# Attention 1 with unscaled probabilities and one division per pair of heads

## The chip, the cores and the metric

One Trainium2 chip, one core. The metric is device time in microseconds of one launch, median of several runs; the profile is one more execution, recorded by the hardware profiler. Engines are called PE (matmul), PEld (its weight loads), DVE (VectorE), ACT (ScalarE), POOL (GpSimd) and SP (SyncE, which only issues weight DMAs here).

## The reference

512 positions, width 1024, float32 throughout. A first block (adaptive modulation, token mixer, convolutional feed-forward) is followed by two more layers (windowed attention with a sink, then latent attention), each with a gated side input. The change lies in the token mixer's attention: 8 heads of 64, chunks of 64 positions, each query sees its own chunk and the 8 before it.

```python
z = h @ w_in + b_in
q, k, v, glu_a, glu_b, gate_a, gate_b = jnp.split(z, splits, axis=-1)
scores = einsum(qc, kb) * HEAD_DIM ** -0.5 + bias      # masked with -1e30
probs = softmax(scores, axis=-1)
out = einsum(probs, vb)
a = out.reshape(b, s, D_ATTN) @ w_attn_o
u = causal_dwconv(glu_a * sigmoid(glu_b), w_dw, b_dw)  # 31 taps, 512 channels
cb = silu(layer_norm(u, g_ln, b_ln)) @ w_conv_o + b_conv_o
y = sigmoid(gate_a) * a + sigmoid(gate_b) * cb
```

The value's share of `b_in` is a constant per channel; rows of `probs` sum to one, so it may be added to v or to `out`.

## The kernel before

All activations stand with channels on the 128 partitions and the 512 positions along the free dimension. Every matmul product is made of three (`mm3`, L610 to L612): each operand is split into a high part in fp32r and the low rest, and hi*hi, hi*lo and lo*hi are added in PSUM. Weights stream from HBM in chunks of 128x1024 by SP's queue; for each chunk ACT makes the high part (`split`, L1029) and then DVE the low one (L1484). PE waits for DVE's count.

The first attention runs in `pair_attention`, a loop over 32 steps (8 heads times 4 query tiles of 128), written out once for each engine and tied by semaphores. Steps go in pairs: step i even and i+1 are the two heads of a pair at the same query tile t; tile t has t+1 key tiles of 128, so widths run 128, 128, 256, 256, 384, 384, 512, 512 and then again. Eight steps finish one pair of heads. What each engine does, by step i:

- PE: at even i the scores of both heads (`pair_scores`, L702), which need the maxima up to step i-1; then two blocks of the gates' matmul (`first_gates`); then the product with the values of step i-5 for odd tiles (`half_values`); then the transposes of the probabilities of step i-3 (`turn`, L732), which wait for the scaled probabilities and for DVE's lo of step i-5; then two more gate blocks. Four blocks a step make one gate tile in two steps, 16 tiles in all. After step 17 `conv_mean` (L817) and after steps 21 and 23 `conv_square` (L824) sum over channels for the layer norm.
- DVE: at even i the masked, biased, negated scores and their minimum for step i (`pair_maxima`, L1587); the reciprocal of the sum of step i-1 (`inverse`, L1599); the low part of the turned probabilities of step i-3 (`pair_turn_lo`, L1615); at odd i the scaling of the probabilities of step i-1 (`norms`, L1609); at even i the maxima of step i+1; at i = 9, 13, ... half an output out of PSUM with the value bias added (`out1`, L1728, two instructions); then `mixer_step`: at even i the low half of a weight chunk, and two of the convolution's taps (`conv_taps`, L1561, 33 of them fall into this loop, the last at step 16) or parts of the layer norm; at i = 15, 23, ... the low part of a finished pair's output (`out1_lo`, L1497).
- ACT: the high part of the turned probabilities of step i-3 (`pair_turn_hi`, L1112); the exponential of step i with its row sum (`exps`, L1087); at even i the scaling of the probabilities of step i-1 (`norms`, L1098); then at even i a gate's tanh (L1239) and a weight chunk's high part (L1029), at odd i a product for the modulation (`ada_product`, L1249); every eighth step the high part of a pair's output (L1034).
- POOL: adds the products of ACT, 128x1024 each, into an accumulator (L520), one in each odd step, and fetches the next.

So even-numbered steps' probabilities are scaled by DVE and odd-numbered ones' by ACT, both in place and before they are turned.

PSUM has 8 banks: 4 and 5 hold scores, 6 and 7 turned probabilities. The other four (`LIN`) are a ring: every output tile of PE takes the next bank in the order in which tiles are finished (`mixer_tiles` for this loop), and `free_bank` makes its first matmul wait until the tile four places earlier has been read. The list `evicted` holds, tile by tile, the semaphore and count that tell so.

The third attention (`attention3`) already leaves its probabilities unscaled: ACT writes the row sums to `lsum`, DVE inverts those of two heads in one instruction (`invert_sums`), copies each over 64 columns (`spread_inverses`, L2032, a 128x512 copy), PE turns that in four transposes (`inverses`, L990) and DVE multiplies the pair's output by the turned inverses out of PSUM (`normalise`, L2040).

## Time and profile before

| | us |
|---|---|
| median of 3 runs (two of them 1616.49 and 1616.67, one 2873.28) | 1616.67 |
| the profiled execution | 1618.08 |
| span of its instructions | 1616.3 |
| PE busy | 1468.8 (91%) |
| DVE busy | 988.3 (61%) |
| ACT busy | 732.9 (45%) |
| POOL busy | 236.7 (15%) |
| PE on the chain that ended last | 70% |
| first attention, from its first scores (198.4) to its last values (365.5) | 167.1 |

Busy time counts an instruction from its start to its modelled end; matmuls overlap, so a PE that is busy all the time can still have slack inside it. The chain that ended last is followed back from the last instruction to whatever released each step. The two sound runs agree within 0.2 us, and the profiled one took 1.4 us more than they.

### The profile page before, as it was taken

What the parts mean: (1) busy time and instruction counts of PE and PEld (TensorE: products, weight loads), DVE (VectorE), ACT (ScalarE), POOL (GpSimd) and SP (SyncE); (2) the same over time, 40 slices, a digit from 0 to 9 for tenths busy, and PEclk for the clock granted to TensorE, in tenths of its full rate; (3) what the DMA queues carried; (4) which work ended last, traced back from release to release, by engine and by line L of the source; (5) the groups of instructions that cost most, each with busy time, mean ns of one, the idle gap of its engine ahead of it and who ended that gap; (6) DMA issues with size and microseconds to landing.
All of it is one profiled execution on the core that took longest, in us unless ns stands there. A gap on an engine that the chain in (4) does not pass through costs nothing.

```text
span 1616.3 us, 19654 instructions
## 1 busy us (share of the span) xinstructions
PE 1468.8 (91%) x6834; PEld 1156.0 (72%) x6834; DVE 988.3 (61%) x1549; ACT 732.9 (45%) x1265; POOL 236.7 (15%) x218
## 2 busy tenths in 40 slices
PE   5898797979987999999998999998999989999897
PEld 3686575767765888887885677776777768778775
DVE  5669878465755555554223647984562568788454
ACT  4424454562324455454123426774442446666442
POOL 3105623231110000000000000111110012222111
PEclk8999799988998999999999999998999999999999
DMA  9532133324621232323322321112222120000221
GB/s 388 192 103 88 56 105 111 110 92 172 219 78 28 102 101 80 104 85 99 102 91 65 98 91 60 59 47 92 80 90 79 55 89 14 27 27 27 105 80 64
DMA packets 39881, 151.65 MB, mean 94 GB/s; under 512 B 4784, under 2 KB 4928, under 8 KB 39040
## 3 DMA queue, kind: packets, MB, share of 16 engines
q1 hardware_dynamic: 29664, 105.92, 20.0%
q0 software_dynamic: 10144, 44.76, 7.6%
q8 instruction: 45, 0.74, 0.2%
q14 instruction: 28, 0.23, 0.0%
HBM read 144.37 MB, written 6.29 MB: 93 GB/s over the span
## 4 chain that ended last, share of the span: by engine, by line
PE 70%; DVE 16%; ACT 7%; issue 5%; DMA 1%; DVEq 0%; POOL 0%; ACTq 0%; SPq 0%; POOLq 0%
PE ps L610 21%; PE ps L611 20%; PE ps L612 20%; DVE w_lo L1484 2%; PE ps L732 2%; PE ps L667 2%; DVE c_acc L1561 2%; ACT w_hi L1029 2%; DVE p L1609 1%; PE ps L702 1%; DMA w_raw<-in_w 1%; PE ps L687 1%; DVE minus_s L1587 1%; DVE pt_lo L1615 1%; DVE tmp L1688 1%
## 5 line engine op out<-in xcount | busy, mean ns | idle before, releaser
L610 PE MATMUL ps<-a_hi,w_hi 128*128 128x512 f32 x880 | 362.3, 412 | 19.7 <-ACTq L1308 11.8
L611 PE MATMUL ps<-a_lo,w_hi 128*128 128x512 f32 x880 | 351.1, 399 | 0.0
L612 PE MATMUL ps<-a_hi,w_lo 128*128 128x512 f32 x880 | 351.0, 399 | 0.0
L1484 DVE TENSOR_TENSOR w_lo<-w_raw,w_hi 128x1024 fp32r<-128x1024 f32 x130 | 166.4, 1282 | 159.6 <-ACT w_hi L1029 158.9
L610 PEld LDWEIGHTS ps<-a_hi,w_hi 128*128 128x128 f32 x880 | 167.9, 191 | 63.6 <-ACTq L1308 12.7
L612 PEld LDWEIGHTS ps<-a_hi,w_lo 128*128 128x128 f32 x880 | 167.6, 190 | 40.2
L611 PEld LDWEIGHTS ps<-a_lo,w_hi 128*128 128x128 f32 x880 | 167.9, 191 | 35.4 <-issue 0.5
L1029 ACT ACTIVATE w_hi<-w_raw 128x1024 fp32r<-128x1024 f32 x138 | 144.4, 1048 | 70.9 <-PE ps L612 55.0
L610 PE MATMUL ps<-b_hi,w_hi 128*128 128x512 f32 x240 | 99.3, 414 | 10.5 <-DVE b_lo L1858 5.6
L611 PE MATMUL ps<-b_lo,w_hi 128*128 128x512 f32 x240 | 96.6, 403 | 0.0
L612 PE MATMUL ps<-b_hi,w_lo 128*128 128x512 f32 x240 | 96.5, 402 | 0.0
L732 PE MATMUL ps<-ident,p 128*128 128x128 f32 x496 | 84.2, 282 | 10.7 <-DVE p L1609 10.4
L1561 DVE SCALAR_TENSOR_TENSOR c_acc<-u_pad,vecs,c_acc 128x512 f32<-128x512 f32 x90 | 85.5, 999 | 0.2
L732 PEld LDWEIGHTS ps<-ident,p 128*128 128x128 f32 x496 | 59.1, 142 | 29.7 <-DVE p L1609 14.0
L1044 ACT ACTIVATE sq<-x_resid 128x512 f32<-128x512 f32 x56 | 35.2, 631 | 98.9 <-DVE x_resid L1937 62.9
L1824 DVE SCALAR_TENSOR_TENSOR c_gate<-u_ff,vecs,c_gate 128x512 f32<-128x512 f32 x44 | 32.9, 748 | 64.4 <-ACT u_ff L1329 64.4
L610 PE MATMUL ps<-g_hi,w_hi 128*128 (+1 forms) x176 | 69.5, 395 | 1.5 <-issue 1.5
L611 PE MATMUL ps<-g_lo,w_hi 128*128 (+1 forms) x176 | 69.4, 394 | 0.0
L612 PE MATMUL ps<-g_hi,w_lo 128*128 (+1 forms) x176 | 69.4, 394 | 0.0
L536 POOL TENSOR_TENSOR sq<-sq 128x512 f32<-128x512 f32 x30 | 38.8, 1293 | 185.9 <-ACT sq L1044 185.9
L1615 DVE TENSOR_TENSOR pt_lo<-ps,pt_hi 128x256 fp32r<-128x256 f32 (+3 forms) x96 | 45.8, 478 | 31.5 <-ACT pt_hi L1112 31.4
L610 PEld LDWEIGHTS ps<-b_hi,w_hi 128*128 128x128 f32 x240 | 46.3, 193 | 24.1 <-issue 6.7
(306 smaller groups left out, 2999.8 us busy)
## 6 DMA issues: line engine op xcount, KB each, us to landing
w_raw<-in_w SPq DMA_DIRECT2D x198, 512.0 KB, 3.5
ada_a<-in_ada POOLq DMA_DIRECT2D x16, 512.0 KB, 7.8
ada_g<-in_ada POOLq DMA_DIRECT2D x16, 512.0 KB, 3.8
ada_b<-in_ada POOLq DMA_DIRECT2D x16, 512.0 KB, 4.3
x_resid<-in_x POOLq DMA_DIRECT2D x2, 2048.0 KB, 11.9
pl_store<-pl_out POOLq DMA_DIRECT2D x2, 2048.0 KB, 8.7
pl<-pl_store POOLq DMA_DIRECT2D x2, 2048.0 KB, 8.7
alibi<-in_alibi POOLq DMA_DIRECT2D x16, 192.0 KB, 2.7
```

The source lines that it names most:

```text
L536: pool.tensor_tensor(sq[:, 0, :], sq[:, 0, :], sq[:, 1, :], ALU.add).then_inc(sq_used, 1)
L610: pe.matmul(o, w[0], r[0], start=start, stop=False, skip_group_check=skip)
L611: pe.matmul(o, w[0], r[1], start=False, stop=False, skip_group_check=skip)
L612: return pe.matmul(o, w[1], r[0], start=False, stop=stop, skip_group_check=skip)
L667: pe.matmul(ps[:, STAT_BANK, :], ones[:, :], sq[:, q % 2, :], start=(k == 0), stop=(k == n - 1)).then_inc(sq_used, 1)
L732: m = pe.transpose(ps[:, T_BANK + n % 2, P * s:P * s + P], a.p[:, n % 4, a.p_at + P * (s - b):a.p_at + P * (s - b) + P], ident[:, :])
L1029: act.activation(w_hi[:, n % SLOTS, :], w_raw[:, n % RAW, :], ACT.Copy).then_inc(w_hi_done, 1)
L1044: act.activation(sq[:, slot, :], src, ACT.Square).then_inc(sq_ready, 1)
L1484: dve.tensor_tensor(w_lo[:, n % SLOTS, :], w_raw[:, n % RAW, :], w_hi[:, n % SLOTS, :].bitcast(F32), ALU.subtract).then_inc(w_lo_done, 1)
L1561: dve.scalar_tensor_tensor(c_acc[:, f, :], src, w, c_acc[:, f, :], ALU.mult, ALU.add).then_inc(conv_step, 1)
L1615: dve.tensor_tensor(lo_, ps[:, T_BANK + n % 2, turned].rearrange("p (s q) -> p s q", q=P), hi.bitcast(F32), ALU.subtract).then_inc(pt_read ...
L1824: dve.scalar_tensor_tensor(c, u_ff[:, 2 * pair + j, tap:tap + TOK], vecs[:, bass.ds(i * 2 + (VO["w_dwf"] + tap * 2 * FT + w_at + pair), 1) ...
```

## The change

It takes the third attention's way of dividing over to the first. Shared helpers get the attention as an argument (`inverses`, `invert_sums`, `spread_inverses`); for the first, the row sums go to `lsum`, DVE inverts a pair's at the end of step 8, 16, 24, 32, spreads them at the end of step 9, 17, 25, 33, PE turns them at the end of step 11, 19, 27, 35, and DVE multiplies at step 13, 21, 29, 37. `inverse` and `norms` stay in the second attention only. The value bias is added by ACT with the high part and again by DVE with the low part. PE's turn now waits for the exponential itself.

```diff
-LN_SUM, LN_SUB, LN_SQUARE, LN_SCALE, LN_OUT = 17, 19, 20, 25, 28
+LN_SUM, LN_SUB, LN_SQUARE, LN_SCALE, LN_OUT = 17, 18, 20, 25, 28
@@ mixer_tiles
+        if i % 8 == 3 and i >= 11:
+            order.append(("l", i // 8 - 1))
@@ eviction of the first attention's tiles
-            evicted.append({"o": (R["o1_half"], j // 2 + 1) if j % 2 == 0 else (tmp_w, tmps_ahead + j // 2 + 1), "g": (R["gate_t"], j + 1), "mean": (R["ln_mean"], CT),
+            evicted.append({"o": (R["o1_half"], j + 1), "l": (tmp_w, tmps_ahead + j + 1), "g": (R["gate_t"], j + 1), "mean": (R["ln_mean"], CT),
@@ attn1 (where the spread inverses stand, by pair)
+                     lambda pair: tile1["l", pair], lambda pair: rs[:, (0, 2, 0, 1)[pair], :], 0)
@@ PE, turn
-                elif n % 2 == 1:
-                    pe.wait_ge(p_ready_act, n // 2 + 1)
+                elif a is attn1:
+                    pe.wait_ge(e_done, n + 1)
                 else:
-                    pe.wait_ge(p_ready, n // 2 + 1)
+                    pe.wait_ge(p_ready_act if i % 2 else p_ready, i // 2 + 1)
@@ PE, pair_attention
                     after(i)
+                    if a is attn1 and i % 8 == 3 and i >= 11:
+                        inverses(a, i // 8 - 1)
@@ ACT, exps and pair_attention
+                least, total = col[:, 0, c:c + 1], col[:, 1, c:c + 1] if a is attn2 else lsum[:, h // 2 % 2, h % 2, t:t + 1]
+                if a is not attn2 and t == 0 and h % 2 == 0 and h >= 4:
+                    act.wait_ge(l_inv, a.pairs_ahead + h // 2 - 1)
-                    if 0 <= i - 1 < a.steps:
+                    if a is attn2 and 0 <= i - 1 < a.steps:
                         norms(a, i - 1)
@@ ACT, high part of a pair's output: Copy becomes Identity with the value bias
+                act.activation(qk_hi[:, pair, :], tmp[:, tmps[0] % 2, :], ACT.Identity, bias=v("b_in", BI_V + pair)).then_inc(hi_done, 1)
@@ DVE, pair_maxima in the second attention
-                        if h >= 2:
-                            dve.wait_ge(e_done, n - 1)
+                    if i >= 2:
+                        dve.wait_ge(e_done, n - 1)
@@ DVE, pair_attention
-                    if 0 <= i - 1 < a.steps:
-                        inverse(a.n0 + i - 1)
+                    if a is attn2 and 0 <= i - 1 < a.steps:
+                        inverse(a, i - 1)
...
-                    if 0 <= i - 1 < a.steps:
+                    if a is attn2 and 0 <= i - 1 < a.steps:
                         norms(a, i - 1)
...
+                    if a is attn1 and i % 8 == 5 and i >= 13:
+                        divide1(i // 8 - 1)
                     after(i)
+                    if a is attn1 and i % 8 == 0 and i >= 8 and i <= a.steps:
+                        invert_sums(a, i // 8 - 1)
+                    if a is attn1 and i % 8 == 1 and i >= 9:
+                        spread_inverses(a, i // 8 - 1)
@@ DVE, out1 (tensor_scalar with the bias becomes tensor_copy), out1_lo
+                    m = dve.tensor_copy(tmp[half(h), tmps[0] % 2, q], src[half(h), 2 * P * h:2 * P * h + 2 * P])
+                dve.scalar_tensor_tensor(qk_lo[:, pair, :], tmp[:, (tmps[0] - 1) % 2, :], v("b_in", BI_V + pair),
+                                         qk_hi[:, pair, :].bitcast(F32), ALU.add, ALU.subtract).then_inc(R["o1"], 1)
@@ DVE, new
+            def divide1(pair):
+
+                inv = bank(attn1.inv(pair))
+                dve.wait_ge(R["o1_half"], 2 * pair + 2)
+                slot = tmp_slot()
+                dve.tensor_tensor(slot, slot, inv, ALU.mult).then_inc(tmp_w, 1)
```

`LN_SUB` is the first of the two steps in which DVE subtracts the mean from the convolution's result (two channel tiles in each).

## Rows read from the trace of the kernel before

**Rows 1.** Windows, core 0, stages of the first attention: busy us (count), TensorE clock, DMA.
```profile
198.00:282.00 84.00, 72.13 (x355) 55.54 (x356) 64.03 (x125) 42.58 (x86) 22.00 (x18) 0.95 0.31 101
...
288.00:330.00 42.00, 42.00 (x225) 32.67 (x226) 22.13 (x52) 25.14 (x49) 9.41 (x7) 1.00 0.28 90
330.00:357.00 27.00, 19.60 (x105) 14.83 (x105) 18.82 (x43) 18.59 (x36) 8.25 (x5) 0.97 0.35 117
357.00:372.00 15.00, 11.51 (x50) 10.45 (x51) 5.30 (x12) 6.01 (x10) 3.99 (x4) 0.50 0.30 105
```

**Rows 2.** Timeline of ACT inside one loop: start us, us, engine, line, op, names, shape.
```profile
266.06 0.72 ACT L1087 ACTIVATE p<-p,col 128x512 f32<-128x512 f32 x1 [6.71 <-DVE col L1587]
...
266.79 0.60 ACT L1098 ACTIVATE p<-p,col 128x384 f32<-128x384 f32 x1
267.29 0.66 ACT L1239 ACTIVATE x_resid<-ps,halves 128x512 f32<-128x512 f32 x1
267.86 1.05 ACT L1029 ACTIVATE w_hi<-w_raw 128x1024 fp32r<-128x1024 f32 x1
```

**Rows 3.** Timeline of DVE, an earlier stall and then the same loop.
```profile
258.35 3.76 DVE L1561 SCALAR_TENSOR_TENSOR c_acc<-u_pad,vecs,c_acc 128x512 f32<-128x512 f32 x2
...
268.94 1.23 DVE L1484 TENSOR_TENSOR w_lo<-w_raw,w_hi 128x1024 fp32r<-128x1024 f32 x1 [1.91 <-ACT w_hi L1029]
270.08 1.53 DVE L1561 SCALAR_TENSOR_TENSOR c_acc<-u_pad,vecs,c_acc 128x512 f32<-128x512 f32 x2
271.53 0.16 DVE L1599 RECIPROCAL col<-col 128x1 f32<-128x1 f32 x1
271.61 0.54 DVE L1615 TENSOR_TENSOR pt_lo<-ps,pt_hi 128x384 fp32r<-128x384 f32 x1
272.06 2.23 DVE L1609 TENSOR_SCALAR p<-p,col 128x512 f32<-128x512 f32 x1
274.21 1.53 DVE L1561 SCALAR_TENSOR_TENSOR c_acc<-u_pad,vecs,c_acc 128x512 f32<-128x512 f32 x2
...
276.25 0.28 DVE L1587 CUSTOM_DVE_ANT_0 p<-ps,rel 128x128 f32<-128x128 f32 x1
```

**Rows 4.** Timeline of POOL over the same stretch.
```profile
259.17 2.38 POOL L520 TENSOR_TENSOR acc_g<-acc_g,ada_g 128x1024 f32<-128x1024 f32 x1 [6.81 <-ACT ada_g L1249]
...
271.64 2.37 POOL L520 TENSOR_TENSOR acc_g<-acc_g,ada_g 128x1024 f32<-128x1024 f32 x1 [9.21 <-ACT ada_g L1249]
```

**Rows 5.** Lines by form, ACT, 198 to 360 us: count | busy us, mean ns | idle.
```profile
L1098 ACT ACTIVATE p<-p,col 128x512 f32<-128x512 f32 x4 | 2.8, 711 | 3.0 <-DVE col L1599 3.0
...
L1098 ACT ACTIVATE p<-p,col 128x128 f32<-128x128 f32 x4 | 1.6, 388 | 0.0
```

**Rows 6.** Lines by form, DVE, 198 to 360 us.
```profile
L1609 DVE TENSOR_SCALAR p<-p,col 128x512 f32<-128x512 f32 x4 | 7.3, 1813 | 0.0
```

**Rows 7.** Tile sq in the third attention: count, duration ns min/median/max, first and last start.
```profile
L990 PE MATMUL ps<-ident,sq x32: 269/272/277, 1355.7 to 1504.8; 128*128 128x128 f32 x32
...
L2032 DVE COPY sq<-gvec x8: 416/418/420, 1351.4 to 1502.8; 128x512 f32<-128x512 f32 x8
```

**Rows 8.** Tile o_pair in the third attention.
```profile
L2040 DVE TENSOR_TENSOR o_pair<-o_pair,ps x8: 676/678/686, 1363.0 to 1505.4; 128x512 f32<-128x512 f32 x8
```

**Rows 9.** Timeline of PE at three places, with idle time before in brackets.
```profile
281.23 3.75 PE L817 MATMUL ps<-c_acc,ones 128*128 128x512 f32 x4 [4.82 <-issue]
...
304.24 1.88 PE L824 MATMUL ps<-sq,ones 128*128 128x512 f32 x4
...
356.90 1.11 PE L732 MATMUL ps<-ident,p 128*128 128x128 f32 x4 [6.32 <-DVE p L1609]
```

**Rows 10.** Timeline of DVE where PE runs without a pause.
```profile
305.26 0.41 DVE L1615 TENSOR_TENSOR pt_lo<-ps,pt_hi 128x256 fp32r<-128x256 f32 x1
305.58 0.41 DVE L1609 TENSOR_SCALAR p<-p,col 128x384 f32<-128x384 f32 x1
305.91 0.97 DVE L1728 TENSOR_SCALAR tmp<-ps,vecs 64x256 f32<-64x256 f32 x2
```

More of the change, by code:

```diff
@@ L417, in build @@
                      lambda h, s: (vb_hi[:, s, P * (h // 2):P * (h // 2) + P], vb_lo[:, s, P * (h // 2):P * (h // 2) + P]),
-                     p3, (pt3_hi, pt3_lo), full, lambda h: tile3["o", h], [[(s, 0, 2) for s in range(4)], [(s, 2, 4) for s in range(4)]])
+                     p3, (pt3_hi, pt3_lo), full, lambda h: tile3["o", h], [[(s, 0, 2) for s in range(4)], [(s, 2, 4) for s in range(4)]],
+                     lambda pair: tile3["l", pair], lambda pair: sq[:, pair % 2, :], H1 // 2)
         used_at = {}
@@ L733, in turn, with inverses @@
                 m.then_inc(t_done, 1)
+            def inverses(a, pair):
+                o = free_bank(a.inv(pair))
+                pe.wait_ge(l_rows, a.pairs_ahead + pair + 1)
+                for t in range(NT):
+                    m = pe.transpose(o[:, P * t:P * t + P], a.spread(pair)[:, P * t:P * t + P], ident[:, :])
+                m.then_inc(lin_done, 1)
             def pair_attention(a, after, between=None):
@@ L983, in value_tile @@
                 m.then_inc(lin_done, 1)
-            def inverses(pair):
-                o = free_bank(tile3["l", pair])
-                pe.wait_ge(R["l_rows"], pair + 1)
-                for t in range(NT):
-                    m = pe.transpose(o[:, P * t:P * t + P], sq[:, pair % 2, P * t:P * t + P], ident[:, :])
-                m.then_inc(lin_done, 1)
             def own_head(h):
@@ L1003, in mla_piece @@
                     elif kind == "l":
-                        inverses(head)
+                        inverses(attn3, head)
                     else:
@@ L1593, in maxima3, with inverse, invert_sums, spread_inverses @@
                 dve.tensor_reduce(col[:, 0, n % 4:n % 4 + 1], ps[:, S_BANK + n % 2, :], AX.X, ALU.max, negate=True).then_inc(m_ready, 1)
-            def inverse(n):
-                c = n % 4
+            def inverse(a, i):
+                n = a.n0 + i
                 dve.wait_ge(e_done, n + 1)
-                dve.reciprocal(col[:, 2, c:c + 1], col[:, 1, c:c + 1]).then_inc(r_ready, 1)
+                dve.reciprocal(col[:, 2, n % 4:n % 4 + 1], col[:, 1, n % 4:n % 4 + 1]).then_inc(r_ready, 1)
             def norms(a, i):
+                if i % 2:
+                    return
                 n = a.n0 + i
-                if n % 2 == 1:
-                    return
                 b, e = a.spans[a.step(i)[1]]
                 p = a.p[:, n % 4, a.p_at:a.p_at + P * (e - b)]
-                dve.wait_ge(r_ready, n + 1)
+                dve.wait_ge(r_ready, i + 1)
                 dve.tensor_scalar(p, p, col[:, 2, n % 4:n % 4 + 1], None, ALU.mult).then_inc(p_ready, 1)
+            def invert_sums(a, pair):
+                dve.wait_ge(*((s_free, 2 * NT * (pair + 1)) if a is attn3 else (e_done, a.n0 + 2 * NT * (pair + 1))))
+                if pair >= 2:
+                    dve.wait_ge(l_rows, a.pairs_ahead + pair - 1)
+                dve.reciprocal(linv[:, pair % 2, :, :], lsum[:, pair % 2, :, :]).then_inc(l_inv, 1)
+            def spread_inverses(a, pair):
+                dve.wait_ge(l_inv, a.pairs_ahead + pair + 1)
+                if pair >= 2:
+                    dve.wait_ge(lin_done, a.inv(pair - 2) + 1)
+                dve.tensor_copy(a.spread(pair).rearrange("p (t e d) -> p t e d", t=NT, e=2),
+                                linv[:, pair % 2, :, :].rearrange("p e t -> p t e").unsqueeze(3).to_broadcast([P, NT, 2, HD])
+                                ).then_inc(l_rows, 1)
             def pair_turn_lo(a, i):
@@ L1724, in out1 @@
             def out1(j):
-                src, c = bank(attn1.lin(j)), VO["b_in"] + BI_V + j // 2
+                src, q = bank(attn1.lin(j)), slice(2 * P * (j % 2), 2 * P * (j % 2) + 2 * P)
                 for h in range(2):
-                    m = dve.tensor_scalar(tmp[half(h), tmps[0] % 2, 2 * P * (j % 2):2 * P * (j % 2) + 2 * P],
-                                          src[half(h), 2 * P * h:2 * P * h + 2 * P], vecs[half(h), c:c + 1], None, ALU.add)
-                m.then_inc(tmp_w if j % 2 else R["o1_half"], 1)
-                tmps[0] += j % 2
+                    m = dve.tensor_copy(tmp[half(h), tmps[0] % 2, q], src[half(h), 2 * P * h:2 * P * h + 2 * P])
+                m.then_inc(R["o1_half"], 1)
             def out1_lo(pair):
-                lo_of_tmp(qk_lo[:, pair, :], qk_hi[:, pair, :], R["o1"])
+                his[0] += 1
+                dve.wait_ge(hi_done, his[0])
+                dve.scalar_tensor_tensor(qk_lo[:, pair, :], tmp[:, (tmps[0] - 1) % 2, :], v("b_in", BI_V + pair),
+                                         qk_hi[:, pair, :].bitcast(F32), ALU.add, ALU.subtract).then_inc(R["o1"], 1)
             def mixer_step(i):
```

59 lines of the change are left out of this document (24 added, 35 removed).

## The prediction

> **What bounds the kernel now.** I read the windows first, then the timelines of ACT, DVE and POOL inside a loop of the first attention, then the groups by form. The windows (columns: stretch, its length, busy us of PE, PEld, DVE, ACT, POOL with counts, TensorE's clock as a share of 2.4 GHz, DMA) cut the attention into four stages [rows 1]. From 198 to 282 us, steps 0 to 17, PE is busy 72 of 84 us, so it has holes; from 288 to 330, steps 18 to about 27, it is busy all 42; from 330 to 357 it has holes again, 7.4 us; from 357 to 372 it runs at 0.50, that is at 1.2 GHz. The change can gain only where PE has holes, and anything that it gives PE to do or to wait for between 288 and 330 counts in full.
>
> What makes the holes is a loop between ACT and DVE, two steps long. ACT waits 6.71 us for DVE's maxima, then does the exponential (266.06), scales the odd step's probabilities (266.79), does a gate's tanh (267.29) and a weight chunk's high part (267.86) [rows 2]. DVE waits for that chunk: its low part starts at 268.94, then two taps, a reciprocal, a lo, the scaling of the even step's probabilities (272.06), two more taps, and the next maxima at 276.25 [rows 3]. So one turn of 10 us has one of ACT's scalings and one of DVE's in it. What DVE does ahead of its wait of 1.91 us (the other reciprocal, the other lo) is covered.
>
> **DVE against POOL.** The scaling at 272.06 took 2.23 us. POOL's addition ran from 271.64 to 274.01, and DVE's next instruction began at 274.21 [rows 3, 4]. The same width costs 1.8 us on average [rows 6], a 384 wide one away from POOL 0.41 [rows 10]. A pair of taps at 258.35 took 3.76 us instead of 1.53, and POOL was adding from 259.17 to 261.55 [rows 3, 4]. The lo of 271.61, which reads PSUM, took its usual 0.54 beside the same addition. So what is held is an instruction whose inputs are all in SBUF, and it is held whichever it is. With the scaling gone, the tap behind it is held until 274.01. Such a place gives 0.2 us, not 2.2. The rows stand for four such scalings (steps 4, 6, 8, 14) and two such pairs of taps (steps 10, 12) up to 282 us. The Trainium skill says the same in "SBUF — State Buffer", section "Who interferes with whom": a single-input VectorE instruction in a two-port mode, or one with two SBUF inputs, and GpSimd lock each other out for a whole instruction. Were the hold the scaling's own, the four held ones of this stretch would give 7 us more, and the sum below would be 1604; the trace bears out the rule.
>
> **The sum, part by part.**
>
> Steps 2 to 17 (until the taps end and PE can sum the mean), gains. ACT's scalings last 388 ns at width 128 and 711 at 512 [rows 5]; neighbours overlap by 0.1 (266.79 plus 0.60 is 267.39, the next starts at 267.29 [rows 2]). That is 0.29 to 0.61, mean 0.45, times 8: 3.6 us. DVE's scalings on the path are 7: three unheld ones at about 0.33 (305.58 to 305.91 [rows 10]), four held ones at 0.2: 1.8 us. At step 9 the half output, which reads PSUM, moves up beside POOL's addition: 0.5 us. Reciprocals on the path: 271.53 to 271.61 is 0.08 [rows 3], times 7: 0.6 us. Together 6.5.
>
> Costs in the same stretch, all on DVE in the loop: an inversion of 8 columns at step 8, like a reciprocal, 0.15; a spread at step 9, 0.42 in the third attention [rows 7], 0.35 behind another; a division at step 13, 0.68 in the third attention [rows 8], 0.6 behind another. Together 1.1. Net gain to the mean: 5.4 us. The tensor_copy for the tensor_scalar of the half output, and the bias in ACT's and DVE's last instructions, keep shape and engine: nothing. The spread reads and writes SBUF, so it can be held by POOL's 2.4 us like the scaling was; at step 9 it stands behind two taps, after the addition, and I count nothing. Bounds of the four spreads: 0.35 each, or 0.42 plus 2.4 each.
>
> PE must still keep up. It is idle 4.82 us before the mean [rows 9] and for the rest of its 12 us of holes before that [rows 1]; 5.4 us fit. Four transposes of 272 ns each, overlapping to some 0.13 apart, are 0.5 us per pair [rows 7]; those of step 11 fall into a hole.
>
> The mean. PE's idle time before it stays near 4 us, because DVE and ACT set both its ends. The clock should fall there as before. I count no change.
>
> Steps 18 to 24, PE without a hole. The four transposes of step 19 cost 0.5. Then the ring. The new tile of each pair takes a bank, and is freed by DVE's division, so the tile four places later waits for it: that is the third pair's first output half at step 15 (tile 11 behind 7), the variance at step 21 (19 behind 15), and the seventh half at step 31 (27 behind 23). At step 21 PE came to the squares at 304.24 [rows 9]; DVE's lo was at 305.26 and its half output at 305.91, 0.97 long [rows 10]. In the new order DVE no longer subtracts two means in step 20 (1.2 us, moved to 18) and ACT has no scaling (0.5), but PE's own turn is 0.5 late: lo at about 304.2, half output to 305.5, division to 306.15. PE arrives at 304.24 + 0.53 = 304.8. It waits 1.4 us. With `LN_SUB` at 18 the mean's bank is free as PE wants it at step 20, within 0.3 us; with 19 it would be a step late. Cost of the stretch: 1.9 us. Bounds of the wait: 0, if DVE comes earlier, and 3, if POOL's addition holds DVE ahead of it.
>
> At steps 15 and 31 PE waits 1.5 us more for its bank, but after both it has a hole of that size or more: in step 16 it needs DVE's maxima, as ACT does at 266.06 [rows 2], and after step 32 it stood idle for 6.32 us [rows 9]. Nothing. If that cover went, it would be 1.5 each.
>
> Steps 24 to 31, the loop bounds again. Each turn gives ACT's 0.3 to 0.5, DVE's 0.2 to 0.33 and a reciprocal. Against them stand the inversion and spread at steps 24 and 25, and the division at 29. Turn by turn: 0.1, 0.6, 0.2. Gain 0.9.
>
> Tail. PE waited until 356.90 for the scaling at step 30 [rows 9], and again until ACT had scaled step 31. Both waits go; late next is the lo of step 29, behind a held `out1_lo` on DVE (the addition of POOL holds that one in the scaling's stead, so 0.25 earlier). The last turns come 1.2 us earlier and the values follow; the last transposes (0.5 to 0.9 at this clock) and the last division (0.65) come onto the chain that ends with `out1_lo` and releases the next stage. Net gain 1.2.
>
> Second attention: one more wait per step in front of the maxima, always satisfied, since the reciprocal of the step before has waited for the same count: nothing. Third attention: the spread waits for PE's transposes two pairs back instead of its own multiply: nothing.
>
> Sum: 5.4 - 1.9 + 0.9 + 1.2 = 5.6 us. From the profiled execution's 1618.1 that gives 1612.5; that execution stood 1.4 above the median of 1616.67, from which the same sum gives **1611.1 us**. That is 0.35%; about 2% is what a measurement of this kernel can tell from no change.
>
> **The rivals.**
>
> *The clock stays up.* PE's pause at 350.6 shrinks from 6.32 us to about 4, and what runs from 357 to 372 at 1.2 GHz may then run at 2.4. For it: the pause shrinks. Against it: in the same stretch PE is busy in small pieces only, and the pause before the mean hardly shrinks. PE is busy 11.5 us there [rows 1], half of which would go, less what waits for others: some 4.5 us, 1606.5; with the mean's stretch as well (the four matmuls of the row at 281.23 take 3.75 us [rows 9], all eight some 7, and half would go), 1603.
>
> *The ring of banks decides: slower.* Each division holds a bank that PE wants two or three steps later, and it comes behind a lo and a half output on DVE. If PE's holes are not where I put them, the three waits (1.5 each), the transposes (2.1), the four spreads and inversions (2.0) and the last division (0.65) all land: 9.3 us against gains of 6.5 + 1.5 + 0.5 = 8.5. Time 1617.5. One held spread makes it 1620. It decides from the point at which PE's waits for its bank add up to more than 0.8 us per turn of the loop, what ACT and DVE save in one. For it: in steps 18 to 24 PE has no hole at all. Against it: DVE waits 1.9 us for ACT even in a loop turn that it bounds.
>
> *Nothing moves.* The loop's saving is eaten by POOL's additions: they start a fixed time after ACT's product, and if DVE comes earlier, its taps start inside them more often, each held up to 2.2 us. Two such would leave 1615.
>
> **How the numbers follow.** Forecast as summed, 1609 to 1614: 0.55. Clock up: 0.15. Ring, slower: 0.15. Nothing moves: 0.15. The range for 8 in 10 leaves out the best end of the clock's case and the worst of the ring's: 1604 to 1618. Over 2% is 32 us, several times every gain or cost named here: faster 0.01, slower 0.01, within 0.98.
>
> **What would show it.** Right: no L1609 or L1098 before 900 us; the mean's matmuls start near 276 instead of 281; the taps behind a lo now show the 2 us that the scalings had; a wait of 1 to 1.5 us before the first squares, released by DVE's division; the pause of 6.3 us down to about 4. Wrong: spreads longer than 0.5 us; pauses of PE at steps 15 or 31 that end later than the loop does; scores still 10 us apart in steps 6 to 16; a different clock between 357 and 372.

## The result, and the profile after

| | before | after | |
|---|---|---|---|
| median, us | 1617.35 | 1607.49 | -9.9 |
| lowest and highest | 1615.1 to 1618.5, and one of 2873.28 | 1606.81 to 1609.37 | six runs each |
| ratio | | 0.9944 | 95% interval 0.9930 to 0.9958 |
| profiled execution | 1618.08 | 1606.92 | -11.2 |
| span, mean granted clock | 1616.3, 0.956 | 1605.1, 0.963 | |

One of the six runs of before took 2873.28 us; the median of before counts it and the ratio does not, so the gain is 9.9 by the medians and 9.1 by the ratio. In the later comparisons before had medians of 1617.2 to 1618.8. The forecast was 1611.1, with a gain of 5.6, and within 2% of no change; so it is, and the interval leaves out no change.

The windows of [rows 1] for the kernel after (columns as there):

```profile
198.00:282.00 84.00, 78.55 (x374) 59.30 (x373) 63.09 (x107) 39.33 (x78) 26.21 (x23) 0.92 0.37 117
288.00:330.00 42.00, 39.50 (x207) 29.87 (x206) 20.82 (x43) 23.99 (x44) 9.35 (x7) 1.00 0.31 101
330.00:357.00 27.00, 21.85 (x122) 18.04 (x120) 19.77 (x36) 16.79 (x32) 10.63 (x6) 0.87 0.30 98
357.00:372.00 15.00, 12.02 (x54) 10.28 (x54) 4.54 (x9) 4.04 (x7) 1.62 (x3) 0.77 0.28 105
```

PE does 78.5 us of work up to 282 us instead of 72.1. The stage without holes begins and ends earlier, so the window of 288 to 330 now has the first of the next stage's. And the last window runs at 0.77 of the full clock instead of 0.50: in before the clock was at its lower level from 355.6 to 376.0, in after from 347.7 to 354.5 and from 361.4 to 368.2. In the first window it is the other way round, 0.92 for 0.95: after lost it in the mean (below) and from 259.0 to 265.8, at the end of a wait for the division at step 15:

```profile
259.48 0.55 PE L617 MATMUL ps<-pt_hi,v_hi 128*128 128x256 f32 x1 [2.81 <-DVE tmp L1801]
```

Before waited 1.26 us at that place. Nothing on DVE waits for PE between there and the mean, so the 1.55 more fell into a hole.

The same loop of DVE as in [rows 3], five microseconds earlier, from its timeline:

```profile
264.93 1.53 DVE L1572 SCALAR_TENSOR_TENSOR c_acc<-u_pad,vecs,c_acc 128x512 f32<-128x512 f32 x2
266.38 0.55 DVE L1643 TENSOR_TENSOR pt_lo<-ps,pt_hi 128x384 fp32r<-128x384 f32 x1
266.85 3.47 DVE L1572 SCALAR_TENSOR_TENSOR c_acc<-u_pad,vecs,c_acc 128x512 f32<-128x512 f32 x2
...
274.42 0.74 DVE L1572 SCALAR_TENSOR_TENSOR c_acc<-u_pad,vecs,c_acc 128x512 f32<-128x512 f32 x1
...
275.75 0.84 DVE L1762 COPY tmp<-ps 64x256 f32<-64x256 f32 x2
276.63 1.23 DVE L1635 COPY rs<-gvec 128x512 f32<-128x512 f32 x1
```

And POOL's two additions of that stretch:

```profile
266.58 2.40 POOL L527 TENSOR_TENSOR acc_g<-acc_g,ada_g 128x1024 f32<-128x1024 f32 x1 [8.83 <-ACT ada_g L1260]
...
275.24 2.34 POOL L527 TENSOR_TENSOR acc_g<-acc_g,ada_g 128x1024 f32<-128x1024 f32 x1 [5.39 <-ACT ada_g L1260]
```

The scaling is gone, and the pair of taps behind the lo takes 3.47 us instead of 1.53: its first tap is held until the addition ends at 268.98, as the scaling of 272.06 was in [rows 3]. The half output at 275.75 (L1762, out of PSUM) runs beside the next addition in its usual 0.84; the spread behind it (L1635, SBUF to SBUF) takes 1.23 instead of 0.42.

PE around the mean, before the squares and at the last turns, from its timeline:

```profile
275.26 5.37 PE L834 MATMUL ps<-c_acc,ones 128*128 128x512 f32 x8 [2.64 <-issue]
```

```profile
298.94 1.98 PE L841 MATMUL ps<-sq,ones 128*128 128x512 f32 x4 [1.39 <-DVE tmp L1801]
```

```profile
348.18 1.09 PE L739 MATMUL ps<-ident,p 128*128 128x128 f32 x4 [2.29 <-DVE pt_lo L1643]
351.43 0.87 PE L739 MATMUL ps<-ident,p 128*128 128x128 f32 x3 [2.16 <-DVE pt_lo L1643]
```

The mean starts at 275.3 instead of 281.2. The wait of 1.39 us for the division is new. The 6.32 us in front of the turn of step 30 [rows 9] have become 2.29 and 2.16, both until a lo of DVE. DVE at that place:

```profile
347.48 0.55 DVE L1643 TENSOR_TENSOR pt_lo<-ps,pt_hi 128x384 fp32r<-128x384 f32 x1
347.94 2.87 DVE L1768 SCALAR_TENSOR_TENSOR qk_lo<-tmp,vecs,qk_hi 128x512 fp32r<-128x512 f32 x1
350.73 0.55 DVE L1643 TENSOR_TENSOR pt_lo<-ps,pt_hi 128x384 fp32r<-128x384 f32 x1
```

The `out1_lo` at 347.94 takes 2.87 us instead of 0.75 behind POOL's addition, and the lo on which PE waits stands behind it.

How the lead over before grew, each place read from PE's timeline in both kernels:

| place | before | after | lead | lead without the 0.9 of the start | forecast |
|---|---|---|---|---|---|
| first scores | 198.4 | 197.4 | 0.9 | 0 | 0 |
| mean's matmuls | 281.2 | 275.3 | 6.0 | 5.1 | 5.4 |
| scores of step 18 | 287.8 | 280.6 | 7.3 | 6.4 | 5.4 |
| scores of step 24 | 315.7 | 310.5 | 5.2 | 4.3 | 3.5 |
| maxima of step 30 (DVE) | 347.9 | 342.0 | 5.9 | 5.0 | 4.4 |
| first product of the next stage | 368.0 | 360.0 | 8.0 | 7.1 | 5.6 |
| end of the span | 1616.3 | 1605.1 | 11.2 | 10.3 | 5.6 |

The 0.9 us at the start counts as scatter: kernels that do not differ up to there had their first scores between 197.4 and 199.1.

### The profile page after: what moved, and what is told of

Its sections match the earlier page's. It is cut to its first block, busy times and chain, and to the rows that moved or that the text cites. A ratio compares the mean times of both kernels' runs of the same rounds, so it can differ in the third digit from the quotient of the medians.

```text
span 1605.1 us, 19696 instructions
## 1 busy us (share of the span) xinstructions
PE 1464.9 (91%) x6850; PEld 1153.0 (72%) x6850; DVE 984.4 (61%) x1513; ACT 726.8 (45%) x1249; POOL 236.5 (15%) x218
## 4 chain that ended last, share of the span: by engine, by line
PE 69%; DVE 16%; ACT 7%; issue 6%; DMA 1%; POOL 0%; DVEq 0%; ACTq 0%; SPq 0%; POOLq 0%
PE ps L617 21%; PE ps L618 20%; PE ps L619 20%; PE ps L739 2%; DVE w_lo L1495 2%; ACT w_hi L1038 2%; DVE c_acc L1572 2%; PE ps L674 1%; PE ps L709 1%; DMA w_raw<-in_w 1%; DVE minus_s L1599 1%; DVE p L1621 1%; PE ps L694 1%; DVE tmp L1722 1%; DVE a_lo L1727 1%
## 5 line engine op out<-in xcount | busy, mean ns | idle before, releaser
L617 PE MATMUL ps<-a_hi,w_hi 128*128 128x512 f32 x880 | 362.0, 411 | 20.6 <-ACTq L1319 11.8
L1572 DVE SCALAR_TENSOR_TENSOR c_acc<-u_pad,vecs,c_acc 128x512 f32<-128x512 f32 x90 | 91.8, 1068 | 0.2
L1120 ACT ACTIVATE pt_hi<-ps 128x256 fp32r<-128x256 f32 (+3 forms) x96 | 41.0, 427 | 53.2 <-PE ps L739 53.0
```

The source lines that it names most:

```text
L617: pe.matmul(o, w[0], r[0], start=start, stop=False, skip_group_check=skip)
L1120: act.activation(hi, ps[:, T_BANK + n % 2, turned].rearrange("p (s q) -> p s q", q=P), ACT.Copy).then_inc(pt_hi_done, 1)
L1572: dve.scalar_tensor_tensor(c_acc[:, f, :], src, w, c_acc[:, f, :], ALU.mult, ALU.add).then_inc(conv_step, 1)
```

## The experiments

Eleven kernels ran beside before, and one more at the end; kernels on the same chip shared their runs of before. The table is for looking up; the runs follow in the order of the questions.

| run | median, us | ratio to before, 95% |
|---|---|---|
| x1_removal | 1604.39 | 0.9922 (0.9907 to 0.9937) |
| x2_act_load | 1616.96 | 1.0003 (0.9990 to 1.0016) |
| x3_dve_load | 1614.97 | 0.9984 (0.9974 to 0.9993) |
| x4_squares_later | 1607.25 | 0.9939 (0.9927 to 0.9951) |
| x5_before_small_adds | 1600.90 | 0.9900 (0.9885 to 0.9914) |
| x6_after_small_adds | 1599.17 | 0.9887 (0.9873 to 0.9902) |
| x7_filler | 1605.41 | 0.9925 (0.9912 to 0.9939) |
| x8_filler_squares | 1602.77 | 0.9907 (0.9893 to 0.9922) |
| x9_before_filler | 1612.47 | 0.9969 (0.9959 to 0.9980) |
| x10_adds_at_maxima | 1597.56 | 0.9877 (0.9862 to 0.9892) |
| x12_before_adds_at_maxima | 1601.53 | 0.9903 (0.9888 to 0.9918) |
| x11_all | 1590.95 | 0.9835 (0.9819 to 0.9852) |

### What the removal and the additions are worth

**x1_removal** takes the scalings and reciprocals out and adds nothing: no inversion, no spread, no turned inverses, no division, so that the first attention's outputs stay unscaled. The mean is subtracted at step 19 again, and the ring of banks is that of before.

```diff
-                        inverses(a, i // 8 - 1)
...
-                        divide1(i // 8 - 1)
...
-                        invert_sums(a, i // 8 - 1)
-                        spread_inverses(a, i // 8 - 1)
```

> Scalings and reciprocals of the first attention are left out and nothing is put in their place (no inversion, spread, transposes or division, so this attention's outputs stay unscaled; mean subtracted at step 19 and the bank ring as before). Theory: what the change adds costs 1.1 us in steps 2 to 17, 1.9 in steps 18 to 24 (half of it a wait of PE for the variance's bank), about 1.1 in steps 24 to 31 and 1 in the tail, so this is 4 to 5 us faster than the changed kernel: about 1603 us, and PE shows no pause before the first squares. Rival, the additions are hidden: as fast as the changed kernel, 1607 to 1608.

Measured 1604.39: 3.1 us under after, where 4 to 5 were expected. Counted from the first scores, its lead over after in the profile is 0.9 at the mean, 2.6 at the scores of step 18, 4.7 at step 24 and 5.8 at the first product of the next stage. But 1.7 of that are the clock inside the mean, whose eight matmuls take 5.37 in after:

```profile
274.70 3.67 PE L830 MATMUL ps<-c_acc,ones 128*128 128x512 f32 x8 [3.37 <-issue]
```

Without it the additions cost 0.9 before the mean (1.1 forecast), 2.1 up to step 24 (1.9) and 1.1 behind (some 2). Of the lead, 2.6 are lost again behind the attention, where the code is the same but for a wait in the third attention; see the clock below.

**x2_act_load** is after with ACT's 16 scalings put back as work without use (same widths and places, into a scratch tile of bfloat16); **x3_dve_load** is after with DVE's 16 scalings and 32 reciprocals put back in the same way.

```diff
+                    if a is attn1 and i % 2 == 0 and 0 <= i - 1 < a.steps:
...
+                        act.activation(scr[:, 0:wd], a_hi[:, 0, 0:wd].bitcast(F32), ACT.Copy, scale=c_act[:, 0:1]).then_inc(scr_done, 1)
```

```diff
+                        dve.reciprocal(col[:, 2, i % 4:i % 4 + 1], ones[:, 0:1])
...
+                        dve.tensor_scalar(scr[:, 0:wd], a_hi[:, 0, 0:wd].bitcast(F32), c_act[:, 0:1], None, ALU.mult)
```

> The changed kernel with ACT's 16 scalings put back as work that nobody waits for (same widths and place, read from another tile, written to a spare one in bfloat16). Theory: ACT's scaling lies on the loop between ACT and DVE; 3.6 us back in steps 2 to 17 and about 1.5 in steps 24 to 31: 1612 us, scores of step 16 some 3.5 us later. Rival, ACT's share was covered by DVE and only PE's waits counted: no change, 1607 to 1608.

> The changed kernel with DVE's 16 scalings and 32 reciprocals put back as work that nobody waits for (written to a spare tile in bfloat16). Theory: an instruction that POOL's addition holds gives its hold over to the next one with its inputs in SBUF, so putting the scalings back costs only their own 0.2 to 0.33 and the reciprocals 0.08: 2.5 to 3.5 us, 1611, while the summed time of the taps falls by about the 5 to 8 us that the put-back scalings show above 0.4 each. Rival, the hold is the scaling's own: 8 us or more, 1616, with the taps as long as in the changed kernel.

At the mean both came as expected: it starts 3.1 us later than in after with ACT's load (3.6 forecast) and 2.9 later with DVE's (2.5 to 3.5). At the end they cost 9.5 and 7.5 (6.5 by the ratios), where some 5 and 3.5 were expected: the totals lie near the rivals of both forecasts. Together they are far more than the whole change gave: the two gains are not a sum, and with either load back most of the whole is gone. DVE's timeline in x3_dve_load, the same loop again:

```profile
267.47 1.53 DVE L1573 SCALAR_TENSOR_TENSOR c_acc<-u_pad,vecs,c_acc 128x512 f32<-128x512 f32 x2
...
269.45 2.34 DVE L1668 TENSOR_SCALAR scr<-a_hi,c_act 128x512 bf16<-128x512 f32 x1
271.71 1.53 DVE L1573 SCALAR_TENSOR_TENSOR c_acc<-u_pad,vecs,c_acc 128x512 f32<-128x512 f32 x2
```

The load's scaling at 269.45 takes the hold of POOL's addition (2.34 us), and the pair of taps behind it is back at 1.53. From the start of the first pair of taps to the end of the second it is 5.77 us here, 5.66 in before and 5.39 in after: the held scaling and its reciprocal cost 0.3 to 0.4 us and not 2.2. The same holds over the whole loop. These are the 33 taps of after and of x3_dve_load, as groups by form from 198 to 360 us (count, busy us, mean ns, idle):

```profile
L1572 DVE SCALAR_TENSOR_TENSOR c_acc<-u_pad,vecs,c_acc 128x512 f32<-128x512 f32 x33 | 34.3, 1068 | 0.2
```

```profile
L1573 DVE SCALAR_TENSOR_TENSOR c_acc<-u_pad,vecs,c_acc 128x512 f32<-128x512 f32 x33 | 28.1, 878 | 0.2
```

Six holds of taps in after are two in x3_dve_load, and the taps take 6.2 us less, as expected (5 to 8); 28.1 and 878 are also their numbers in before. This is shown, then: the hold passes to what follows.

What is beyond 3 us comes behind that. x2_act_load is 3.6 late at the scores of step 18, 5.8 at step 24, 7.0 at step 30 and 10 past the first product of the next stage; its profiled execution, 1621.07, was one of the slower of its runs (1613.09 to 1621.62), so that its profile shows more than the median. PE's time for the mean's eight matmuls is 6.69 us in before, 5.37 in after, 5.92 and 6.07 in these two, and 3.67 in x1_removal. The pause before the squares is 1.79 us in x2_act_load instead of 1.39, and the clock falls in the squares (303.4 to 306.8): the four matmuls take 3.51 us instead of 1.98.

### POOL's additions

**x5_before_small_adds** and **x6_after_small_adds**: before and after, with POOL adding 8 columns of 1024, which leaves the modulation incomplete.

```diff
-                    pool.tensor_tensor(acc[:, :], acc[:, :], ada_g[u % 2][:, :], ALU.add).then_inc(ada_g_used, 1)
+                    pool.tensor_tensor(acc[:, 0:8], acc[:, 0:8], ada_g[u % 2][:, 0:8], ALU.add).then_inc(ada_g_used, 1)
```

> The kernel before, with POOL's 14 additions for the modulation cut from 1024 to 8 columns (the modulation of two groups comes out incomplete). Theory: the holds go, 1.7 to 2.2 us at each of six places up to 282 us, but PE's own 8 us a turn then bounds: the mean 7 to 9 us earlier, 2 more at the layer norm's scaling and 2 at the last scalings: 1604 to 1607. Rival, the holds were covered: above 1612.

> The changed kernel with the same cut additions. Theory: the changed kernel is held at the same six places, by its taps, so it gains too, but it is nearer to PE's bound: the mean about 5 us earlier, 2 each at the layer norm's scaling and at the low part of the third pair's output: 1597 to 1600, 5 to 8 us below the kernel before with cut additions. Rival, holds belonged to the scalings: it gains under 3 us, 1605, and the change is worth nothing without POOL's additions.

Before fell by 16 us (10 to 13 were expected) and after by 8.3, so that only 1.7 us lie between them (the intervals of the two ratios overlap) instead of 5 to 8. Without the holds the scalings cost before little: its mean starts 71.9 us after the first scores, against 70.5 in x6_after_small_adds, 77.8 in after and 82.9 in before. PE's window in x6_after_small_adds says why (columns as in [rows 1]):

```profile
198.00:282.00 84.00, 81.90 (x419) 63.50 (x421) 57.44 (x118) 44.04 (x87) 10.29 (x23) 0.97 0.37 122
288.00:330.00 42.00, 40.60 (x211) 30.56 (x210) 22.38 (x47) 26.60 (x50) 3.03 (x8) 1.00 0.31 102
```

PE is busy 81.9 of 84 us, it bounds the stage, and what DVE saves behind it buys little. In the profiles x6_after_small_adds leads x5_before_small_adds by 1.5 at the mean, 3.1 at the scores of step 18 (1.7 of it the mean's clock), 0.6 at those of step 30 and, with the shorter pauses of the tail, 4.0 at the first product of the next stage. So 8 to 16 us of the kernel hang on the holds, more than on the scalings.

**x10_adds_at_maxima** keeps all additions and all other work and only places them: POOL waits until the maxima of the step are through before it adds, so that its 2.4 us lie under DVE's reading of PSUM and its wait for ACT. **x12_before_adds_at_maxima** is the same wait in before.

```diff
                 if k:
+                    pool.wait_ge(*((m_ready, 2 * u + 5) if u < 14 else (pt_ready, NT * H1)))
```

> The changed kernel with each of POOL's additions held back until the maxima of the next even step are done (and the last two until the last low part is), so that they run while DVE reads PSUM and waits for ACT. All work stays. Theory: the holds go as with the cut additions; up to 1599.2 as measured there, less what still meets a tap: 1600 to 1602. Rival: an addition of 2.4 us behind the maxima now holds the weight chunk's low part, 1.9 us behind them, in every turn: no gain, 1607, or a little slower.

> The kernel before with the same placing of POOL's additions. Theory: both kernels lose their holds, and with PE as the next bound the change is worth only 2 us (as with the cut additions): 1601 to 1604, 1 to 3 above the changed kernel with the same placing. Rival: the scalings are what the additions hold whatever their place: above 1610.

After fell by 9.9 to 1597.56, more than expected, before by some 16 to 1601.53. POOL's and DVE's timelines in x10_adds_at_maxima:

```profile
256.15 2.40 POOL L528 TENSOR_TENSOR acc_g<-acc_g,ada_g 128x1024 f32<-128x1024 f32 x1 [7.18 <-issue]
...
264.03 2.40 POOL L528 TENSOR_TENSOR acc_g<-acc_g,ada_g 128x1024 f32<-128x1024 f32 x1 [4.61 <-issue]
```

```profile
256.26 0.68 DVE L1600 CUSTOM_DVE_ANT_0 p<-ps,rope 128x512 f32<-128x512 f32 x1
...
259.56 1.53 DVE L1573 SCALAR_TENSOR_TENSOR c_acc<-u_pad,vecs,c_acc 128x512 f32<-128x512 f32 x2
...
261.48 1.53 DVE L1573 SCALAR_TENSOR_TENSOR c_acc<-u_pad,vecs,c_acc 128x512 f32<-128x512 f32 x2
...
264.27 0.28 DVE L1600 CUSTOM_DVE_ANT_0 p<-ps,rel 128x128 f32<-128x128 f32 x1
```

The addition of 256.15 runs beside the maxima (out of PSUM, 0.68 us as always) and the wait behind them, and no tap is longer than 0.75 us in the whole loop; in after six are held and take 1.34 to 2.98. In this placing the change is worth 4.0 us, though the intervals of the two ratios still overlap by a little (0.9892 and 0.9888 are their near ends), and the clock is in it: the mean's eight matmuls take 3.67 us in x10_adds_at_maxima, behind a pause of 1.34, and 5.36 in x12_before_adds_at_maxima, behind one of 3.02. The same 1.7 us are part of what the placing gained over after.

### The ring of banks

**x4_squares_later** moves the squares one step later each, so that PE does the next scores while DVE divides.

```diff
-        if i == LN_SQUARE + 3:
+        if i == LN_SQUARE + 4:
             order.append(("var", 0))
...
-                if i in (LN_SQUARE + 1, LN_SQUARE + 3):
-                    conv_square(i - LN_SQUARE - 1)
-                    conv_square(i - LN_SQUARE)
+                if i in (LN_SQUARE + 2, LN_SQUARE + 4):
+                    conv_square(i - LN_SQUARE - 2)
+                    conv_square(i - LN_SQUARE - 1)
```

> The changed kernel with PE's sums of squares one step later (steps 22 and 24), so that the variance's tile comes one place later in the ring of banks and waits for an output half that DVE reads in step 21 before its division. Theory: the pause of 1.4 us before the first squares goes and nothing takes its place; scores of step 24 come 1.4 us earlier, 1606 us. Rival: the wait moves to the next tile (the output half of step 23, whose bank the division frees) or to ACT, which needs the variance in step 24: no gain, 1607 to 1608.

The pause of 1.39 us is gone from the profile, and the lead over after is 1.6 at the turn of step 24 and 3.2 at step 30, counted from the first scores. The median does not show it: 1607.25 against 1607.49, which is the rival's time. The lead is not lost in the attention: it is still 3.3 at the first product of the next stage, and the same code behind takes 3.3 us more than in after, with the clock at its lower level for 76 us instead of 66 (table in the next section). The medians of x8_filler_squares and x7_filler, 2.6 us apart, speak for the same.

### The clock

**x7_filler** gives PE matmuls without use into the scores' bank where it would pause: 9 before the mean, 9 and 8 before the last two turns, 12 behind the last values. **x8_filler_squares** is that with the squares later. **x9_before_filler** is before with 18, 24, 0 and 9 at the same places.

```diff
+            def filler(count, ready):
+
+                pe.wait_ge(m_ready, ready)
+                for _ in range(count):
+                    pe.matmul(ps[:, S_BANK, :], a_hi[:, 0, 0:P], a_hi[:, 0, :], start=True, stop=True)
...
                 if i == LN_SUM:
+                    filler(9, LN_SUM + 1)
                     conv_mean()
```

> The changed kernel with matmuls of no use put into PE's pauses: 9 ahead of the mean, 9 and 8 ahead of the last two turns, 12 behind the last values, each 0.235 us at full clock, written to a scores bank already read. Theory: the pauses stay but the granted clock doesn't fall, so the mean is about 1.7 us shorter and the values, the modulation's matmuls and the first output tile behind the attention run at 2.4 GHz: 4 to 6 us faster, about 1602. Rival, the stages behind the pauses wait for DVE and ACT anyway: within 1 us of the changed kernel; or fillers end later than the pauses and cost up to 2.

> The changed kernel with both the fillers and the later squares. Theory: they touch different stretches, so their gains add: 2 from the fillers as measured and 1.4: 1604. Rival: no more than the fillers alone, 1605.4.

> The kernel before with fillers in its pauses: 18 matmuls ahead of the mean, 24 ahead of the turn at 356.9, 9 behind the last values. Theory: the change gains the 5 to 6 us of its own sum with the clock held up in both, and the rest of the 9 to 10 measured came from the clock, which was low for 6 and 20 us here at the mean and the tail against 3.4, 6.6 and 6.4 in the changed kernel: this runs 5 to 6 us above the changed kernel with fillers (1605.4), at 1611. Rival, the whole gain is the change's own: 1614 or more. Other rival, more than half was clock: 1608 or less.

What they are to mend, microsecond by microsecond in after (PEclk is the third column from the right):

```profile
275.00:276.00 1.00, 0.73 (x2) 0.49 (x3) 1.00 (x4) 0.15 (x1) 0.76 (x1) 1.00 0.38 49
276.00:277.00 1.00, 1.00 (x2) 0.34 (x1) 0.95 (x3) 0.00 (x0) 1.00 (x1) 0.52 0.78 303
...
279.00:280.00 1.00, 1.00 (x3) 0.45 (x2) 0.00 (x0) 0.00 (x0) 1.00 (x2) 0.78 0.74 143
280.00:281.00 1.00, 1.00 (x8) 0.41 (x6) 0.00 (x0) 0.00 (x0) 0.60 (x2) 1.00 0.97 385
```

PE pauses from 272.6 to 275.3, resumes at the full clock, and loses it at 276 in the middle of the mean, until 279.4. In x7_filler the mean's row and the end's window are:

```profile
276.73 3.67 PE L842 MATMUL ps<-c_acc,ones 128*128 128x512 f32 x8 [0.54 <-issue]
```

```profile
340.00:357.00 17.00, 15.63 (x92) 12.67 (x91) 13.51 (x24) 10.05 (x18) 8.69 (x6) 1.00 0.28 95
357.00:372.00 15.00, 14.48 (x80) 12.10 (x79) 7.21 (x13) 4.44 (x7) 2.52 (x6) 1.00 0.43 154
```

The eight matmuls take 3.67 us instead of 5.37, and 340 to 372 runs at 1.00. The median fell by 2.1 where 4 to 6 were expected (its ratio and after's overlap by 0.001). With the squares later as well it fell by 4.7, that is by 2.6 for the squares (the intervals of the two ratios overlap by 0.001). Between before and after, both with fillers (x9_before_filler and x7_filler), lie 7.1 us, by medians and by ratios, instead of 9.1 (ratio) or 9.9 (medians). Each of these medians is uncertain by some 2 us, so the difference of 2.0 to 2.8 is a rough size.

Nor are the two with fillers at an equal clock: they are nearly so in the attention, but not behind it. This is where the time of each profile goes, with the stay at the lower clock summed from the clock records behind the profile's PEclk:

| profile of | first scores to the next stage's first product, us | of it at the lower clock | from there to the end, us | of it at the lower clock |
|---|---|---|---|---|
| before | 169.7 | 26.3 | 1248.3 | 80.9 |
| after | 162.5 | 20.6 | 1245.1 | 66.2 |
| x1_removal | 156.7 | 13.9 | 1247.8 | 79.8 |
| x4_squares_later | 159.2 | 17.2 | 1248.4 | 76.3 |
| x9_before_filler | 164.9 | 7.2 | 1246.9 | 76.9 |
| x7_filler | 160.1 | 10.5 | 1244.1 | 62.5 |
| x10_adds_at_maxima | 149.5 | 7.2 | 1248.8 | 76.8 |
| x11_all | 147.3 | 3.6 | 1243.5 | 62.9 |

In the attention the change gains 7.1 us without fillers and 4.8 with them: 2.3 are the clock there. Behind the attention the change touches two waits only, which the prediction counts as nothing, and yet after is 3.1 us faster than before. All 14 profiles fall into two groups: 1243.5 to 1246.4 us where the clock was at its lower level for 62 to 69 us, and 1246.9 to 1250.5 where for 76 to 83. The lead of after over before grows and shrinks in stretches of PE's work where the two clocks differ: by 1.6 at 424 to 431 and 2.3 at 1101 to 1110, and back by 2 near 960, where after alone lost the clock (948.5 to 951.9). Before at the first two of these places, and after at about the same places of the program:

```profile
423.00:430.00 7.00, 7.00 (x27) 6.03 (x27) 4.88 (x8) 3.43 (x4) 0.75 (x2) 0.56 0.46 156
1099.00:1112.00 13.00, 9.03 (x31) 7.36 (x32) 4.75 (x10) 4.47 (x7) 2.22 (x3) 0.53 0.17 43
```

```profile
414.00:421.00 7.00, 6.89 (x31) 5.87 (x32) 5.23 (x9) 3.08 (x4) 0.53 (x1) 0.76 0.58 176
1090.00:1103.00 13.00, 8.50 (x38) 6.78 (x39) 5.08 (x11) 4.73 (x9) 2.56 (x3) 0.87 0.27 92
```

Why the clock falls for longer in one kernel than in another behind the attention no run shows. But a difference of 3 us between two of these kernels can come from code that both share.

### All together

**x11_all** is x10_adds_at_maxima with the squares later and fillers where x10_adds_at_maxima still paused: 7 before the turn of step 30, 12 behind the last values, none before the mean.

> The change with POOL's additions tied to the maxima (as x10_adds_at_maxima), the squares one step later each (as x4_squares_later), and matmuls without use in two of PE's remaining pauses: 7 in front of the turn of step 30, 12 behind the last values; none in front of the mean, where PE's pause was 1.3 us in x10_adds_at_maxima and the clock did not fall. All the work of the reference is kept. Theory: the three gains stand in different places and add up. x10 measured 1597.56; the pause of 1.39 us in front of the squares goes (-1.5 to -3), and the clock stays up between the last values and the next stage (-2): 1593 to 1595. Rival: with the holds gone PE is the bound from step 18 on and each of its pauses is covered or taken up at a later place by the clock, so that it comes out at 1597 or above, as the squares alone gave nothing in x4_squares_later.

Measured 1590.95 (1589.77 to 1592.17), under the range expected and 1.65% under before. Its windows and its pauses:

```profile
198.00:282.00 84.00, 81.77 (x419) 63.35 (x421) 57.47 (x118) 43.95 (x87) 25.57 (x23) 0.97 0.36 121
288.00:330.00 42.00, 42.00 (x219) 32.07 (x218) 24.52 (x52) 29.39 (x55) 11.82 (x8) 1.00 0.34 113
330.00:357.00 27.00, 24.78 (x143) 21.22 (x143) 13.48 (x27) 12.59 (x21) 9.35 (x7) 0.94 0.26 98
357.00:372.00 15.00, 15.00 (x65) 12.07 (x65) 11.93 (x16) 4.44 (x6) 3.18 (x6) 1.00 0.74 278
```

```profile
338.43 0.39 PE L618 MATMUL ps<-pt_hi,v_hi 128*128 128x256 f32 x1 [0.98 <-DVE pt_lo L1657]
...
346.06 1.14 PE L695 MATMUL ps<-ones,acc_g 128*128 128x1 f32 x9 [1.24 <-issue]
```

PE is busy 163.6 of the 168 us in these windows (151.9 in after; 4.8 of the 163.6 are the fillers), and the pause before the squares is not there. Against x10_adds_at_maxima it leads by 3.3 us at the scores of step 22 (from the first scores) and by 6.1 in the span, though it started 1.2 later. Between 352 and 1308 us that lead changes by no more than 0.4; the last 3 come at 1308 to 1311, 1486 to 1491 and 1585 us, in code that is the same. At these places x10_adds_at_maxima has the clock at its lower level for 6.9 and 6.8 us and from 1583.7 to the end at 1595.7, x11_all for 3.4 and 3.4 us and from 1581.3 to the end at 1589.6. So 2.6 to 4.6 were expected from named places, 3.7 came from them, and the rest goes with the clock behind the attention, which the edit does not touch: it may be luck.

## Why the prediction was right, and where it was not

**Steps 2 to 17: right.** 5.4 forecast, 5.1 measured, and by the mechanism given: the hold passed to the taps (x3_dve_load shows it from the other side), ACT's part and DVE's part came back at the mean as 3.1 and 2.9, and the additions cost 0.9 there (x1_removal) where 1.1 were forecast. One reading was too wide: what is held is not every instruction whose inputs are all in SBUF, for reciprocals are not (last section).

**"The mean. ... I count no change": wrong by 1.3 us.** The argument was that the pause before it hardly shrinks. It shrank from 4.82 to 2.64, because PE came to it only 2.9 us earlier (276.4 and 272.6, less the start) while DVE was 5.1 earlier, and the clock came back inside the mean: 5.37 us for the eight matmuls instead of 6.69. The case in the rivals gave this stretch 3.5; after took 1.3 of it, x7_filler 3.0, which is all that there was.

**Steps 18 to 24: right.** 1.9 forecast, 2.1 measured (6.4 to 4.3), with the wait of 1.4 us before the squares at 1.39. That the mean's bank was no matter at step 20 held too. Without the wait the attention is 3.3 us shorter in the profile of x4_squares_later, and x8_filler_squares is 2.6 faster than x7_filler by the medians; some of both may be the clock.

**The spreads: one in four on a bad place.** They take 0.52, 1.23, 0.41 and 0.97 us, so that one of the signs named for a wrong forecast (spreads over 0.5) came. The 1.23 lies under the mean, where DVE waits 3.35 us for PE afterwards, and costs nothing; the 0.97 at 352.7 lies beside PE's last values, which run until 356.7.

**Steps 24 to 31: right.** 0.9 forecast, 0.7 measured.

**The tail: right in kind, short in size.** The pause of 6.32 was to become 4; it became 2.29 and 2.16 with a turn between. The net gain was to be 1.2 and was 2.1 up to the first product of the next stage, and the clock gave the rest: 0.77 for 0.50 between 357 and 372. I had named both and put a chance of 0.15 on a clock that stays up, with 1606.5; 1607.49 is nearer to that than to 1611.1, and the other sign of a wrong forecast, a different clock between 357 and 372, came too. The term that was mis-sized is the clock's, which the sum puts at nothing. In the profiles it measured 2.3 us in the attention (7.1 gained without fillers, 4.8 with them), and the stages behind, where the sum has nothing either, ran 3.1 us faster with 66 instead of 81 us at the lower clock. So of the 11.2 between the two profiles 4.8 are the change's own, against 5.6 forecast, 2.3 the clock in the attention, 3.1 the stretch behind and 0.9 the start. The mechanism was right. That its net sum came so near is in part luck: by x1_removal the additions cost some 4.1 us and not 5.1, so the gains behind a net of 4.8 must have been too high as well, and the two errors cancel in part.

**The rivals.** The ring did not decide: its wait at step 15 was 1.55 longer than before and at step 31 0.35 long (1.5 counted for each), and both fell into holes. "Nothing moves" needed taps that start inside additions more often. Up to the mean there are six held instructions as in before; the taps of the loop average 1068 ns for it, but that was in the sum already. The part of x5 and x6 that I expected and did not get (5 to 8 us of the change left without holds, 1.7 found) says where the forecast stood on thin ground: its 6.5 us were gains in a loop that POOL's additions had made the bound.

## What to carry to other kernels

When an instruction is held by another engine, taking it away does not take the hold away: price it at what the next in line will not pay, and ask whether the holder can be put under work that it does not disturb. Here that one wait on POOL was worth as much as the change itself (9.9 us, some of it the clock's), and it cost nothing. Count PE's clock as a term of its own wherever the change moves PE's pauses (1.3 to 6.3 us here), in both directions, and take the sizes from the same matmuls at either clock in the trace. And before a difference of a few microseconds is put down to an edit, compare the stages that the edit does not touch: here they differed by 3.3 us between after and x4_squares_later, which have the same code in them.

## What was not expected of the hardware

The clock can fall after a pause has ended: PE paused for 2.64 us, ran from 275.3 at the full clock, and lost it from 276.0 to 279.4. The same pause of 2.64 us before the mean in x4_squares_later, and pauses of 3.02 in x5_before_small_adds and x12_before_adds_at_maxima, left the eight matmuls at 5.3 to 5.4 us; a pause of 3.37 in x1_removal left them at 3.67. So the length of the last pause alone does not decide, and between the two outcomes lie 1.7 us.

The hold between DVE and POOL goes both ways. At 236 us in after, both timelines:

```profile
235.44 1.41 DVE L1572 SCALAR_TENSOR_TENSOR c_acc<-u_pad,vecs,c_acc 128x512 f32<-128x512 f32 x2
236.76 0.20 DVE L1628 RECIPROCAL gvec<-gvec 128x8 f32<-128x8 f32 x1
...
238.31 2.01 DVE L1572 SCALAR_TENSOR_TENSOR c_acc<-u_pad,vecs,c_acc 128x512 f32<-128x512 f32 x2
```

```profile
236.26 2.84 POOL L527 TENSOR_TENSOR acc_g<-acc_g,ada_g 128x1024 f32<-128x1024 f32 x1 [4.61 <-ACT ada_g L1260]
```

The addition took 2.84 us instead of 2.39; a tap was running when it began, and had 0.59 left. The reciprocal of 8 columns inside it took its usual 0.20 and was not held, though it reads and writes SBUF; the tap behind was, until 239.1. Nor were the reciprocals of 128x1 in before: six of them begin inside an addition and take 0.15 or 0.16 us, as outside one, such as that of 230.36 in the addition that runs from 230.07 to 232.71. The Trainium skill ("SBUF — State Buffer", section "Who interferes with whom"), on which the prediction draws, does not have them held either unless they run in a two-port mode: an instruction of VectorE with at most one SBUF input outside these modes does not contend with GpSimd. In which mode a reciprocal runs no run here shows.
